# In the first attention's softmax, VectorE takes a row's reciprocal and scaling one step later

## The reference, cut to what matters

```python
logits = jnp.einsum('bqhd,bqkhd->bqhk', qb, k_sel).astype(jnp.float32) * scale
logits = jnp.where(valid[:, :, None, :], logits, -jnp.inf)
p = jax.nn.softmax(logits, axis=-1)
return jnp.einsum('bqhk,bqkhd->bqhd', p.astype(v.dtype), v_sel)
```

## Time and profile before

| what | before |
|---|---|
| median of 3 runs | 1909.9 us (1908.96 to 1912.99) |
| the profiled execution's own time | 1909.39 us |
| its span | 1907.3 us |
| PE busy | 1829.6 us (96%) |
| DVE busy | 799.9 us (42%) |
| ACT busy | 749.3 us (39%) |
| POOL busy | 777.5 us (41%) |
| chain that ended last, by engine | PE 82%, DVE 10%, ACT 3%, issue 3% |
| the attention steps (first L1789 to last L1779) | 155.1 to 271.2 us of the span |

### The profile page before, as it was taken

How to read it: one execution, slowest core, us unless ns; L and a number is a source line. 1 busy time by engine, 2 the same in 40 slices (tenths; PEclk the granted TensorE clock), 3 DMA queues, 4 the chain that set the end, 5 groups by cost and what they waited for, 6 DMA issues and landing times.

```text
span 1907.3 us, 20381 instructions
## 1 busy us (share of the span) xinstructions
PE 1829.6 (96%) x8018; PEld 1440.3 (76%) x8018; DVE 799.9 (42%) x1389; ACT 749.3 (39%) x1176; POOL 777.5 (41%) x360
## 2 busy tenths in 40 slices
PE   7999999999999999899999999999899899999987
PEld 6687768888888786388888888777677688767665
DVE  3594442211221199732200211587677422245563
ACT  4523344322332366454312332444244332454432
POOL 3343214444444379634444444344444343433211
PEclk9999999999999999999999999999999899999998
DMA  5232113333233232022333332322322232322101
GB/s 184 67 99 78 56 35 93 97 98 100 88 100 99 85 103 78 0 78 88 100 100 99 100 97 91 121 69 77 109 83 73 77 100 69 108 74 66 56 22 44
DMA packets 100094, 160.31 MB, mean 84 GB/s; under 512 B 7296, under 2 KB 30208, under 8 KB 100000
## 3 DMA queue, kind: packets, MB, share of 16 engines
q1 hardware_dynamic: 100000, 159.02, 26.8%
HBM read 156.90 MB, written 2.10 MB: 83 GB/s over the span
## 4 chain that ended last, share of the span: by engine, by line
PE 82%; DVE 10%; ACT 3%; issue 3%; POOL 1%; DMA 1%; SPq 0%; POOLq 0%; DVEq 0%; ACTq 0%
PE bank L585 24%; PE bank L587 24%; PE bank L586 24%; PE bank L834 2%; PE bank L877 1%; POOL w_lo L2319 1%; DVE gla_state L2235 1%; DVE rg_t L2022 1%; DVE rg_t L2033 1%; DVE rg_i L2029 1%; DVE rg_sq L2021 1%; PE bank L665 1%; PE bank L1031 1%; PE bank L1014 1%; ACT prob L1252 1%
## 5 line engine op out<-in xcount | busy, mean ns | idle before, releaser
L2319 POOL TENSOR_TENSOR w_lo<-w_raw,w_hi 128x1024 fp32r<-128x1024 f32 (+1 forms) x286 | 690.2, 2419 | 1075.7 <-ACT w_hi L1129 1075.6
L585 PE MATMUL bank<-x_hi,w_hi 128*128 128x512 f32 (+1 forms) x1264 | 507.7, 402 | 18.1 <-POOL w_lo L2319 16.3
L1129 ACT ACTIVATE w_hi<-w_raw 128x1024 fp32r<-128x1024 f32 (+1 forms) x286 | 299.6, 1054 | 562.2 <-PE bank L587 556.5
L586 PE MATMUL bank<-x_lo,w_hi 128*128 128x512 f32 (+1 forms) x1264 | 494.9, 392 | 0.0
L587 PE MATMUL bank<-x_hi,w_lo 128*128 128x512 f32 (+1 forms) x1264 | 494.6, 391 | 0.0
L585 PEld LDWEIGHTS bank<-x_hi,w_hi 128*128 128x128 f32 (+1 forms) x1264 | 238.3, 188 | 77.8 <-POOL w_lo L2319 17.2
L586 PEld LDWEIGHTS bank<-x_lo,w_hi 128*128 128x128 f32 (+1 forms) x1264 | 238.5, 189 | 54.4 <-issue 5.1
L587 PEld LDWEIGHTS bank<-x_hi,w_lo 128*128 128x128 f32 (+1 forms) x1264 | 238.0, 188 | 52.0 <-issue 0.2
L585 PE MATMUL bank<-w_hi,f_hi 128*128 128x512 f32 x512 | 200.0, 391 | 0.0
L587 PE MATMUL bank<-w_hi,f_lo 128*128 128x512 f32 x512 | 199.3, 389 | 0.0
L586 PE MATMUL bank<-w_lo,f_hi 128*128 128x512 f32 x512 | 199.2, 389 | 0.0
(11 more groups left out here) (270 smaller groups left out, 2081.6 us busy)
## 6 DMA issues: line engine op xcount, KB each, us to landing
w_raw<-in_mlp_w SPq DMA_DIRECT2D x128, 512.0 KB, 3.7
w_raw<-in_even_w_in SPq DMA_DIRECT2D x48, 512.0 KB, 3.8
w_raw<-in_dsa_w_in SPq DMA_DIRECT2D x28, 512.0 KB, 3.6
w_raw<-in_odd_w_in SPq DMA_DIRECT2D x24, 512.0 KB, 3.6
w_raw<-in_conv_w_pw SPq DMA_DIRECT2D x32, 256.0 KB, 3.0
w_raw<-in_even_w_out SPq DMA_DIRECT2D x16, 512.0 KB, 4.2
w_raw<-in_dsa_w_out SPq DMA_DIRECT2D x8, 512.0 KB, 3.8
w_raw<-in_conv_w_pw SPq DMA_DIRECT2D x8, 512.0 KB, 3.7
```

The source lines that it names most:

```text
L585: e.matmul(o, sh, mh, start=first, stop=False)
L586: e.matmul(o, sh, ml, start=False, stop=False)
L1129: e.activation(hi, src, ACT.Copy).then_inc(*w_hi.up(u))
L2319: e.tensor_tensor(lo, src, hi.bitcast(F32), ALU.subtract).then_inc(*w_lo.up(u))
```

## The change

```diff
                 if i < len(ATTENTION):
                     h, t = ATTENTION[i]
-                    n, p, top, total = (t + 1) * P, prob[i % 4], att[:, i % 4, 0:1], att[:, i % 4, 1:2]
+                    n, p, top = (t + 1) * P, prob[i % 4], att[:, i % 4, 0:1]
                     w.wait_ge(*logit.at(h, t))
...
                     w.wait_ge(*biased.at(h, t))
                     e.tensor_scalar(top, top, stat(0, 5, t), None, ALU.mult).then_inc(*scaled_max.up(h, t))
+                if 0 <= i - 1 < len(ATTENTION):
+
+                    h, t = ATTENTION[i - 1]
+                    n, p, total = (t + 1) * P, prob[(i - 1) % 4], att[:, (i - 1) % 4, 1:2]
                     w.wait_ge(*exped.at(h, t))
                     w.wait_ge(*own_dve.after(e.reciprocal(total, total)))
                     e.tensor_scalar(p[:, 0:n], p[:, 0:n], total, None, ALU.mult).then_inc(*prob_out.up(h, t))
```

## The result

The changed kernel took 1917.95 us, the median of 7 runs, against 1912.14 us for 7 runs of the kernel before: a ratio of 1.0039, 95% interval 1.0026 to 1.0051, or 5 to 10 us slower. The ratio compares all runs and not the two medians: the medians lie 5.8 us apart, the means (1911.67 and 1919.23) 7.6 us. A second set of runs later gave 1.0039 again (1.0025 to 1.0054), with means 7.7 us apart. The forecast was 1917.9 us, 8.0 us more than the 1909.9 it started from; since the median of the kernel before came out at 1912.14 with more runs, it is the 8.0 us that is to be compared, and not the 1917.9.

The account below looks back on a forecast made before the run. PE, busy 96% of the span, was taken as the bound. Terms 7.45 + 1.56 - 0.30 - 0.70 = 8.0 us later at row 7, kept to the end, gave 1917.9 us from the median; range 1914.8 to 1922.0.

Parts of the forecast that it names:

- long places: T(13), T(17), T(21), T(25), T(29), with tile 1: PE waits for the later scaling, 1.49 us each, 7.45 us lost.
- middle places: T(15), T(19), T(23), T(27), with tile 3: scaling now behind the copy C, 0.39 us each, 1.56 us lost.
- the tail: T(31) at the attention's end: 1.82 us after T(30) against 2.12 before, a gain of 0.30 us.
- the held S(24): Scaling of step 24, 1.03 us beside POOL's `w_lo`: its delay counted as gained, 0.70 us.
- The chain of the long place: From V(19)'s start through `att_lo`, L1793, reciprocal and scaling to T(21): 3.74 us.
- up to two held scalings: Range allowance for scalings held again beside POOL's work after the change: up to +1.4 us.
- The covered places: Steps 0 to 12, each between two k rows: 4.64 us of PE work covers the 3.74 us chain, cost 0.
- The delay at the end: PE is full behind row 7, so the 8.0 us delay there stays to the end; otherwise the forecast is wrong.
- Faster: Rival: PE loses waits hanging on the exponential in the attention, gaining 3.6 us, 1906.3 us; chance 3%.
- No change: Rival: delay caught up behind 270 us, where PE waits 16.6 us for `w_lo`; up to all returns, 1910; chance 4%.
- that rival: Clock rival: PE's five attention waits of about 2 us lower its clock, up to 14 us more; over 2 us: 6%.
- the waits that I named in advance: PE's nine waits for the scaling between 213 and 272 us: five near 2.0 us, four near 1.05 us.

Follow-up runs that it names:

- steps 0 to 12 later: Against the kernel before, only the scalings of attention steps 0 to 12 come one step later; ratio 1.0006, row 0 to row 7 56.88 us.
- the version with tile 2 later: Against the kernel before, only the scalings of tile 2 (j = 2, 6, 10, ...) come one step later; ratio 0.9977, row 0 to row 7 52.33 us.
- the version with the rows moved: Changed kernel with output-product k rows moved on PE and matching ACT calls, one between V(19) and T(21); ratio 1.0048, row 0 to row 7 65.01 us.
- the version with moved rows and short `w_lo`: Changed kernel with k rows moved, plus POOL's remainder of three products cut to 64 of 1024 columns; row 0 to row 7 61.13 us, one run.

## Why the prediction was right

By its own steps, in the distance of PE from one row to the next:

| term | predicted | measured |
|---|---|---|
| long places, five | 1.49 each, 7.45 | 1.41 each, 7.05 |
| middle places, four | 0.39 each, 1.56 | 0.35 each, 1.40 |
| the tail | -0.30 | +0.16 |
| the held S(24) | -0.70 | -0.65 |
| sum | 8.0 | 7.96 (the two ends give 7.98) |

*The chain of the long place.* From V(19)'s start to T(21) I had 3.74 us; it is 248.14 - 244.40 = 3.74. The unknown interval from L1793 to the reciprocal, taken as 0.12, is 0.13. The price is 0.08 less than mine, mainly because V(20) and the row behind it start 0.14 apart when V(20) hasn't waited for itself, and 0.24 when it has the earlier trace rows. I had left that out.

*The middle place.* T(22) to T(23): 2.26 predicted, 2.28 measured. Against 1.87 before that is 0.41; from row to row 0.35 of it arrives.

*The held scaling.* The 0.65 us was gained by a hair: S(23) started at 253.23, and POOL's remainder beside it ended at 253.25. I had let both come near 252.5; a little earlier, and up to 0.7 us would have been lost again.

*The tail* is the one term with the wrong sign. The chain itself was right, but S(31) took 0.98 us, since POOL's remainder ran beside it; that was in the range ("up to two held scalings") and not in the sum. The miss is 0.46 us, and what I had put too high in the long places (0.40) and the middle ones (0.16) cancelled it. The hit at 0.02 us is luck to that extent. That the median of the changed kernel, 1917.95, also falls on my 1917.9 is luck entirely, since the median before moved by 2.2 us with more runs.

*The covered places* cost nothing: 59.73 us from the first logit product to row 0 with steps 0 to 12 later, 59.74 before and after.

*The delay at the end.* I had named as a sign of being wrong that 8 us at row 7 isn't the delay at the end. Neither profile shows it there (12.6 and 10.3 us of span); the means of the runs do (7.6 and 7.7).

*The rivals.* "Faster" named real waits of PE, and the version with tile 2 later shows them to be worth 4.5 us; what failed in it is its condition, for T(21) could start only 2.85 us after the last product of V(19) (245.29 to 248.14) in place of 0.88. Some 0.65 of the 4.5 is the held scaling, which the rival counted too. "No change" failed: behind row 7 nothing was caught up, and PE's waits for `w_lo` behind it are 16.6 us in both the earlier trace rows. The clock held at 1.00 from 205 to 285 us in the changed kernel, through waits of 1.83 us. But it fell twice in the version with the rows moved, behind waits of 2.45, so that rival lay closer than its 6% suggests. The Trainium skill (TensorE: Matmul & The Clock Gate, HAM oscillation) has the clock fall each time round a loop that leaves TensorE idle. The two falls behind 2.45 us agree with that in kind; the changed kernel, with five waits of 1.82 to 1.83 us and no fall, shows that waits of this size alone don't bring it about.

In the waits that I named in advance, the sizes are 1.82 and 0.91 in the profile where I wrote 2.0 and 1.05: the profile counts idle time from a matmul's modelled end, 0.14 us behind the start of the next one that could have gone.

## What to carry to other kernels

Moving a producer behind other work hides its own wait, but puts that work into the path of whoever consumes it; count from the consumer: how far ahead of its use was the result, and what now stands between. If the pipeline has no slack at that place, move the consumer by the same step, or move only the cases whose wait was on somebody's path: here one scaling in four brought all of the gain between row 0 and row 7 that moving scalings gave. And when a change mixes gaining and losing cases, split it by case before giving it up.

## What was not expected of the hardware

A VectorE scaling that starts while GpSimd works on its weight remainder ends only after that does: 1.03 us for about 0.29 (before), 0.98 for 0.49 (after), 1.87 for 0.42 (rows moved). In the 13 traces here 50 scalings started during a full-width remainder and more than 0.06 us before its end. All 50 ended behind it, by 0.08 to 0.09 us with 128 columns, 0.15 with 256, 0.21 to 0.22 with 384 and 0.28 to 0.29 with 512, whatever their start. That is as if they did all their columns after POOL was through; the traces don't show it from inside. L1789, L1793, the reciprocal and the copy C, started beside the same work, kept their durations. The Trainium skill (GPSIMD Engine Reference, Specifications) gives SBUF interfaces shared with VectorE as the place of such contention. In the kernel before with POOL's work cut to 64 columns, no scaling took more than 0.49.

In the version with moved rows and short `w_lo` the granted clock of TensorE fell in a stretch of small matmuls whose longest waits were 0.99 and 0.91 us (0.79 from 236 to 244 us), yet stayed at 1.00 in the changed kernel with waits of 1.83 us. What tells the two apart these runs don't show.
